# A hybrid decoder trunk on one core: the first mixer's chunk inverses over all four quadrants of TensorE, another order of scores, sums and weighing, and eight element-wise steps more on GpSimd

## What is computed

```python
def step(state, x):
    sa = jnp.einsum('bhij,bhj->bhi', state, a_t)
    state = state * w_t[:, :, None, :] + sa[..., None] * b_t[:, :, None, :] + v_t[..., None] * k_t[:, :, None, :]
    return state, jnp.einsum('bhij,bhj->bhi', state, r_t)
...
y = ((y - mean) * lax.rsqrt(var + RWKV_GN_EPS)).reshape(b_, s_, RWKV_WIDTH)
y = y * gn_w + gn_b
bonus = jnp.sum(r_h * k_h * r_k, -1, keepdims=True) * v_h
y = y.astype(cols.dtype) + bonus.reshape(b_, s_, RWKV_WIDTH)
return y * g
```

## Time and profile before

| | us |
|---|---|
| median of 3 runs | 1387.68 (1383.47 to 1388.83) |
| the profiled execution | 1384.46 |
| its span, first to last instruction | 1382.7 |

### The profile page before, as it was taken

The page is one execution under the profiler, slowest core; times in us unless marked ns, Lnnn a source line. Parts: engine busy times, 40 slices in busy tenths (PEclk is TensorE's granted clock), DMA queues, the critical chain, the costliest instruction groups (busy, mean ns, idle before and its releaser), DMA issues. The chain is left out here.

```text
span 1382.7 us, 20783 instructions
## 1 busy us (share of the span) xinstructions
PE 1252.7 (91%) x8752; PEld 701.5 (51%) x8752; DVE 408.8 (30%) x1019; ACT 269.8 (20%) x537; POOL 15.2 (1%) x18
## 2 busy tenths in 40 slices
PE   7999999899999888598899999998999998877986
PEld 4678874444444433243378888544444453333432
DVE  1158764511112111112135756224211211110211
ACT  2241440311110100010132566112111010000101
POOL 0000000000000000000000111000000000000000
PEclk9999999999999999889999999999999999997999
DMA  9620128999999999999964455958999999999996
GB/s 305 189 95 28 64 82 354 404 428 428 428 425 429 427 427 427 426 426 428 369 219 169 152 212 199 366 230 327 427 428 427 428 427 428 427 426 426 427 428 264
DMA packets 63482, 464.08 MB, mean 336 GB/s; under 512 B 8272, under 2 KB 13680, under 8 KB 34960
## 3 DMA queue, kind: packets, MB, share of 16 engines
q1 hardware_dynamic: 63376, 462.61, 81.8%
HBM read 461.51 MB, written 1.08 MB: 335 GB/s over the span
## 5 line engine op out<-in xcount | busy, mean ns | idle before, releaser
L1982 PE MATMUL bank<-raw,xg 128*32 128x512 f32 x1664 | 233.6, 654 | 46.9 <-DMA raw<-in_moe_w_up 41.1
L1892 DVE TENSOR_TENSOR aT<-bank,sg 128x128 f32<-128x128 f32 (+1 forms) x64 | 20.2, 316 | 553.9 <-ACT sg L1803 553.9
L1982 PEld LDWEIGHTS bank<-raw,xg 128*32 128x32 f32 x1664 | 57.9, 119 | 196.6 <-issue 122.0
L1919 PE MATMUL bank<-sel,ux 128*128 128x64 f32 (+1 forms) x896 | 117.7, 287 | 17.0 <-DVE sel L1825 16.1
L1919 PEld LDWEIGHTS bank<-sel,ux 128*128 128x128 f32 x896 | 110.9, 202 | 40.7 <-issue 21.6
L2029 PE MATMUL sums<-ys,selT 64*128 64x512 f32 x512 | 127.2, 615 | 3.3 <-DVE ys L1905 3.3
L1800 ACT COPY gus<-bank 128x512 f32<-128x512 f32 x64 | 37.5, 586 | 439.5 <-PE bank L1982 332.1
L2020 PE MATMUL bank<-raw,aT 128*32 128x512 f32 x832 | 100.0, 598 | 10.8 <-DVE aT L1892 10.8
L2029 PEld LDWEIGHTS sums<-ys,selT 64*128 64x128 f32 x512 | 44.1, 186 | 87.8 <-issue 80.9
L1963 PE MATMUL bank<-raw,xg 128*64 128x512 f32 x384 | 87.0, 594 | 0.0
L2623 PE MATMUL sums<-uT,wr 128*128 128x256 f32 x352 | 78.1, 380 | 0.0
(11 more groups left out here) (414 smaller groups left out, 1282.4 us busy)
## 6 DMA issues: line engine op xcount, KB each, us to landing
raw<-in_moe_w_gate SPq DMA_DIRECT2D x54, 2048.0 KB, 41.7
raw<-in_moe_w_up SPq DMA_DIRECT2D x54, 2048.0 KB, 46.1
raw<-in_moe_w_down SPq DMA_DIRECT2D x54, 2048.0 KB, 45.0
raw<-in_moe_w_gate SPq DMA_DIRECT2D x20, 1024.0 KB, 11.2
raw<-in_moe_w_up SPq DMA_DIRECT2D x20, 1024.0 KB, 12.7
raw<-in_moe_w_down SPq DMA_DIRECT2D x20, 1024.0 KB, 12.4
wr<-in_ssm_w_in SPq DMA_DIRECT2D x10, 2048.0 KB, 8.1
wr<-in_hyb_w_in SPq DMA_DIRECT2D x5, 2048.0 KB, 7.9
```

What stands on the lines that cost most here:

```text
L1892: V.tensor_tensor(out, bank[TURN_BANK][:, 0:8 * n].rearrange("p (j x) -> p j x", j=4)[:, :, n:2 * n], gated, ALU.mult).then_inc(S["act"], 1)
L1919: i = T.matmul(bank[SIDE_BANK][:, k * n:(k + 1) * n].rearrange("p (x s) -> p x s", x=2), ux[:, t, 4 * half + k, :], src[:, t, :, :], start ...
L1982: i = T.matmul(bank[GU_BANK][CAP_S * c:CAP_S * c + CAP_S, :], xg_f[:, x, 4 * half + k, :], raw[:, slot, k * FH:(k + 1) * FH], start=(half ...
```

## The change

1. `squares` takes both halves at once. For half t=1 tri and triT are kept with the partitions of the two chunks swapped (`crossed`), by a new multiplication "crossed" for triT and by products' output; so products and dT run over all four quadrants, and so do akv and wu. dTT stays with two. The first input of the second half, "at", is turned by eight 64-wide multiplications instead of four transposes.
2. gains of a chunk and queries of the next are given alternately.
3. In each round scores and products come before the turning and the attending; on VectorE the sums come before the weighing, and dT's sums before dTT's; on ScalarE products_read comes before weights_read.
4. The masks of rounds 1 to 4, three steps of pre and one of gate go to GpSimd; VectorE's last part and SyncE's next load wait for the last of them ("gain").

```diff
@@ VectorE, ahead of the rounds
-            did(V.tensor_tensor(triT, nrb[:, :, 0, :], rep(levT[:, 0], SL), ALU.mult))
+            go(V.tensor_tensor(triT[:, 0:HEADS, :], nrb[:, 0:HEADS, 0, :], rep(levT[:, 0], HEADS), ALU.mult))
+            dve.wait_ge(*at("crossed"))
+            for e in range(2):
+                go(V.tensor_tensor(triT[:, slot(1, e, 0):slot(1, e, 4), :],
+                                   bank_of("crossed", e)[:, 0:4 * CHK].rearrange("p (c s) -> p c s", s=CHK),
+                                   rep(levT[:, 0], 4), ALU.mult), "read", "crossed", e)
+            dve.wait_ge(dve_done, DV.n)
@@ VectorE, a round
-            masked(3)
-            dve.wait_ge(*got("par"))
-            go(V.tensor_tensor(pre, pre, rep(gn_b, HALVES), ALU.add))
             compressed_turned(1)
+            grown(3)
             weighted(4)
-            grown(3)
@@ GpSimd
+            def masked(l):
+
+                pool.wait_ge(*(at("prod", l - 1, 1) if l > 1 else at("lvl", 1)))
+                go(G.tensor_tensor(lv[:, (l + 1) % 2], nrb[:, :, 0, :], rep(levT[:, l + 1], SL), ALU.mult), "lvl", l + 1)
+
+            masked(1)
+            masked(2)
+            ...
+            go(G.tensor_tensor(pre, pre, gate[:, :, :], ALU.mult))
+            pool.wait_ge(pool_done, PO.n)
+            go(G.tensor_tensor(gate[:, :, :], gate[:, :, :], rep(gn_w, HALVES), ALU.mult), "gain")
@@ ScalarE, a round
+            products_read(4)
             attention_read(0)
             weights_read(4)
-            products_read(4)
@@ TensorE
-            def squares(b, g, left_, right_):
+            def squares(bs, left_, right_, source, to):
 
-                for s in range(HEADS):
+                for n in range(HEADS):
                     for q in range(2):
-                        i = T.matmul(b[at64(q), s * CHK:(s + 1) * CHK], left_[at64(q), HEADS * g + s, :],
-                                     right_[at64(q), HEADS * g + s, :], start=True, stop=True)
+                        for g in bs:
+                            i = T.matmul(bs[g][at64(to(g, q)), n * CHK:(n + 1) * CHK],
+                                         left_[at64(source(g, q)), HEADS * g + n, :],
+                                         right_[at64(source(g, q)), HEADS * g + n, :], start=True, stop=True)
                 return i
+
+            straight = lambda g, q: q
+            crossed = lambda g, q: q if g == 0 else 1 - q
 
             def products(l):
 
                 pe.wait_ge(*at("lvl", l))
                 if l == 1:
                     pe.wait_ge(*at("triT0"))
+                else:
+                    pe.wait_ge(*at("read", "dT", l - 1, 1))
+                bs = {g: take(pe, "prod", l, g, pool=right) for g in range(2)}
+                squares(bs, lv[:, l % 2], tri, straight, crossed).then_inc(pe_done, PE.one(("prod", l, 1)))
+
+            def grown(l):
+
+                pe.wait_ge(*at("read", "prod", l, 1))
+                if l > 1:
+                    pe.wait_ge(*at("read", "dTT", l - 1, 1))
+                if l < LAST:
+                    bs = {g: take(pe, "dT", l, g, pool=right) for g in range(2)}
+                    squares(bs, triT, prod, crossed, straight).then_inc(pe_done, PE.one(("dT", l, 1)))
                 for g in range(2):
+                    squares({g: take(pe, "dTT", l, g, pool=right)}, prod, triT, crossed, crossed).then_inc(
+                        pe_done, PE.one(("dTT", l, g)))
@@ TensorE, a round
-            weights_turned(4)
             scores(5)
             products(4)
+            attended(1)
+            weights_turned(4)
             grown(4)
@@ TensorE, behind the rounds
-            gains(0)
-            queries(1)
-            gains(1)
+            gains_queries(0)
             pe.wait_ge(*at("read", "wu", 1, 0))
             pe.wait_ge(*at("read", "wu", 1, 1))
-            gains(2)
-            queries(2)
-            queries(3)
+            gains_queries(1)
+            gains_queries(2)
             weights_turned(7)
```

More of the change, by code:

```diff
@@ L571, in _ @@
             sp.wait_ge(*at("attended", 3))
+            sp.wait_ge(*at("gain"))
             load_ahead(sp, 0, hyb_fed, hyb_attended)
@@ L791, in _ @@
                                        rep(pair, 4), ALU.mult), "read", "kar", t, e)
[L793 to L800 removed]
             def grown(l):
[L804 to L807 removed]
+                for name, dst in (("dT", tri), ("dTT", triT)):
+                    if name == "dT" and l == LAST:
+                        continue
+                    for g in range(2):
                         dve.wait_ge(*at(name, l, g))
@@ L1073, in _ @@
             exps(2)
+            products_read(2)
             weights_read(2)
-            products_read(2)
             exps(3)
@@ L1342, in _ @@
             against("bar", bh)
+            bs = [take(pe, "crossed", e, pool=right) for e in range(2)]
+            for c in range(4):
+                for e in range(2):
+                    for q in range(2):
+                        i = T.matmul(bs[e][at64(1 - q), c * CHK:(c + 1) * CHK],
+                                     bh[at64(e), c, chunk(1, q)], ar[at64(e), c, 0, chunk(1, q)], start=True, stop=True)
+            i.then_inc(pe_done, PE.one(("crossed",)))
             pe.wait_ge(*at("rk"))
@@ L1392, in _ @@
             grown(1)
+            scores(3)
+            products(2)
             attended(0)
             weights_turned(2)
-            scores(3)
-            products(2)
             compressed_out(0)
@@ L1436, in _, with gains_queries @@
             pe.wait_ge(*at("read", "at", 1))
-            for t in range(HALVES):
-                pe.wait_ge(*at("read", "dTT", LAST, t))
-                for e in range(2):
-                    b = take(pe, "wu", t, e, pool=right)
-                    for c in range(4):
-                        for q in range(2):
-                            i = T.matmul(b[at64(q), 2 * c * CHK:2 * (c + 1) * CHK], triT[at64(q), slot(t, e, c), :],
-                                         flat(xr_[at64(q), slot(t, e, c), :, :], "x", "s"), start=True, stop=True)
-                    i.then_inc(pe_done, PE.one(("wu", t, e)))
-            def gains(j):
+            pe.wait_ge(*at("read", "dTT", LAST, 1))
+            for e in range(2):
+                bs = [take(pe, "wu", t, e, pool=right) for t in range(HALVES)]
+                for c in range(4):
+                    for q in range(2):
+                        for t in range(HALVES):
+                            half = at64(crossed(t, q))
+                            i = T.matmul(bs[t][at64(q), 2 * c * CHK:2 * (c + 1) * CHK], triT[half, slot(t, e, c), :],
+                                         flat(xr_[half, slot(t, e, c), :, :], "x", "s"), start=True, stop=True)
+                i.then_inc(pe_done, PE.one(("wu", 1, e)))
+                new[("wu", 0, e)] = new[("wu", 1, e)]
+            def gains_queries(j):
                 t, q = j // 2, j % 2
-                b = take(pe, "g", j, pool=right)
+                t2, q2 = (j + 1) // 2, (j + 1) % 2
+                b, b2 = take(pe, "g", j, pool=right), take(pe, "qm", j + 1, pool=right)
                 for c in range(4):
```

117 lines of the change are left out of this document (53 added, 64 removed).

## The result

| | before | after |
|---|---|---|
| median | 1386.66 us (1383.47 to 1388.83, 4 runs) | 1375.51 us (1374.99 to 1377.71, 4 runs) |
| the profiled execution | 1384.46 us | 1377.71 us |
| its span | 1382.7 us | 1375.9 us |

The ratio is 0.9921, with a 95% interval from 0.9899 to 0.9943: faster by 0.8%. The forecast was 1381.3 us with a range from 1376 to 1388. The profiled execution took 1377.71 us where the sum gave 1378.1; the median lies 5.8 us under the forecast and 0.5 us under the range.

The account below looks back on a forecast made before the run. TensorE was taken to bound the rounds, VectorE close behind. Opening +2.2, rounds -9.2, end -0.95 and clock fall +1.6 sum to -6.35 us: 1378.1 for the profiled execution, 1381.3 for the median, range 1376 to 1388.

Parts of the forecast that it names:

- the rounds: First mixer's rounds: four-quadrant overlap and vanished waits, less two new waits, save 9.2 us.
- the akv wait: Round three: dTT wants akv's banks, which ScalarE empties only behind round four's exponentials, a new wait of 1.0 us.
- the new wait: Behind wu: TensorE waits about 2 us in front of the third gains-and-queries call.
- the adding: Opening: VectorE's adding of the identity, held by GpSimd's first mask, takes 2.7 us in place of 1.2.
- The opening, which gets longer: Up to the first scores: GpSimd's hold, crossed reads, turnings and clock add 2.2 us, bounds +0.5 and +3.5.
- The fall behind the new wait: After wu: TensorE's clock falls to half behind the wait before the third gains-and-queries call, costing 1.6 us.
- The base: Starting time: profiled execution 1384.46 us, the median of the runs 1387.68, 3.2 higher, added to the forecast.
- -0.95: End of the mixer: from wu's start to unit 7's turning takes 0.95 us less.
- rival 1: Opening and end: no fall of the clock and no holding, -8 to -10 us, 1378; chance 0.2.
- 2: Rounds: GpSimd also holds VectorE's PSUM-reading instructions, about 1 us per step reaches TensorE, +6, 1387.5 us; chance 0.15.
- 3: Rounds, wu and gains: four quadrants don't overlap because of a shared bank, +1, 1388.7 us; chance 0.07.
- 4: Rounds and opening: GpSimd's 128x1024 steps take longer, 5.5 us each, and delay the weighing, net +9, 1396.5 us; chance 0.08.

Follow-up runs that it names:

- e2: Changed kernel with the halves one after the other, only two quadrants alternating in products, dT, akv and wu: 1380.72 us, ratio 0.9962 to before.
- e6: Changed kernel with masks, bonus (pre) and gate steps back on VectorE: 1377.9 us, ratio 0.9945 to before.
- e3: Changed kernel with GpSimd's first mask waiting for VectorE's adding of the identity: 1375.53 us, ratio 0.993 to before.
- e9: Changed kernel with TensorE's opening waits filled by idle multiplications and GpSimd's first mask behind the identity's adding: 1375.64 us, ratio 0.9928 to before.
- e8: Changed kernel with idle multiplications in TensorE's two opening waits, first mask not moved: 1376.62 us, ratio 0.9939 to before.
- e13: Changed kernel again, no edit, a single profiled execution: 1375.04 us.
- e1: Changed kernel again, no edit, beside the kernel before: 1375.7 us, ratio 0.9935 to before.
- e7: Changed kernel with VectorE's weighing ahead of its sums again in all five rounds: 1379.29 us, ratio 0.9966 to before.
- e12: Changed kernel with e10's two orders, the first mask later, opening unfilled and a shorter filling at the end: 1370.38 us, ratio 0.9892 to before.
- e4: Changed kernel with two idle multiplications ahead of the third gains-and-queries call and two ahead of the last carried step: 1373.78 us, ratio 0.9922 to before.
- e10: Changed kernel with akv read ahead of unit 4's exponentials and unit 7's weights turned before the third gains-and-queries call: 1374.46 us, ratio 0.9916 to before.
- e14: Changed kernel again, no edit, a second single profiled execution: 1372.24 us.
- e5: Kernel before with two idle multiplications ahead of its last carried step: 1383.38 us, ratio 0.9988 to before.
- e11: Changed kernel with e9's filling and later mask, e10's two orders and the end filled: 1372.0 us, ratio 0.9903 to before.

## Why the prediction was right, and where it was wrong

**Right, with its numbers.** That TensorE sets the rounds and VectorE must get shorter with it: e2 and e6 show the two sides. Products 1.09 us forecast as 1.10, dT 0.98 as 1.10, a round of 7.14 us as 7.2, the akv wait 1.07 as 1.0, the turning's wait in round five 0.32 as 0.35 (and one more of 0.30 behind it, not walked), the new wait 1.98 as 2, unit 7's turning at 191.08 as 191.5, the adding 2.60 as 2.7, GpSimd's steps 2.36 us as 2.1 to 2.5. The Trainium skill's rule on banks and row tiles (TensorEngine Tiling (Array Packing), Gotcha 1: PSUM Pressure) would have kept products at 1.92 us; here two row halves wrote one bank, into different partitions, and the products took 1.09. Its rule on the lock (SBUF — State Buffer, Who interferes with whom) held on both sides: 2.60 us beside GpSimd and 1.23 without for two SBUF operands (e3).

**The opening, which gets longer: +2.2 us. Over-sized.** The four profiled executions of the changed kernel give +1.0, +0.75 and twice +0.05 (23.51, 23.23, 22.53, 22.53 against 22.48), 0.5 in the mean. I took GpSimd's hold (1.5) as lying on the path. It does not: TensorE has kar at half clock meanwhile, and e3 takes the hold away without winning anything; where the half clock is short, 0.4 us of it count (e9 against e8). The lower bound of +0.5 was the better value. TensorE's rows of kar (64x128) and of the first turning behind it (128x128) show what the sum left out, before, after and in e13, two rows each:

```profile
129.92 2.47 PE L1322 MATMUL sums<-front,qk 64*64 64x128 f32 x64
134.03 1.97 PE L1155 MATMUL sums<-cst,qk 128*128 128x128 f32 x8 [1.64 <-DVE wr L789]
132.03 3.69 PE L1339 MATMUL sums<-front,qk 64*64 64x128 f32 x64 [0.82 <-DVE kk L788]
135.66 1.97 PE L1172 MATMUL sums<-cst,qk 128*128 128x128 f32 x8
130.06 3.56 PE L1339 MATMUL sums<-front,qk 64*64 64x128 f32 x64 [0.82 <-DVE kk L788]
133.56 1.23 PE L1172 MATMUL sums<-cst,qk 128*128 128x128 f32 x8
```

With "crossed" ahead of it kar starts 2.1 us later behind the start of nn (15.59 and 15.60 against 13.46). Before, the turning waited 1.64 us for VectorE and came 4.11 us behind kar; now it comes 3.63 and 3.50 us behind it without a wait. From the turning to products of round one are 4.94 us before, 4.29 after and 3.43 in e13: with the delay of kar the length of the half clock decides between +1.0 and nothing. Of the eleven executions with the opening not filled six have the long one and 23.2 to 23.5 us (after, e1, e3, e6, e7, e12), five the short one and 22.5 (e2, e4, e10, e13, e14).

**The fall behind the new wait: +1.6 us. The size was right and the certainty wrong.** It is 1.4 to 1.7 us where it comes; it came in one of four profiled executions of the changed kernel (and in those of e3 and e6). It should have stood as a chance of one in four, 0.4 us; with e3, e6, e8 and e9, where the wait is also 1.98 us and nothing fills it, it came in three of eight. What decides whether it comes is not settled: the wait is 1.98 us in all four, with the same work ahead of it, and that it did not come with the wait filled (e4) is one execution. The old fall at the join, which I took for fixed, is missing in one of the four as well.

**The base: 1384.46 to 1387.68, "3.2 higher". Wrong.** I added the whole difference between the profiled execution and a median of three runs. Over 69 runs the median of before is 1385.49, 2.2 us lower.

These account for most of it: 2.2 of the base, 1.7 of the opening, 1.2 of the fall and 0.3 of the missing one at the join, together 5.4 us; the rounds, at 8.7 in place of 9.2, take 0.5 back, which leaves 4.9 of 5.8 us. The executions say the same in another way: mean length of the mixer 117.64 before and 108.26 after, -9.4 us, where my sum was -6.35; 1385.49 - 9.4 = 1376.1, and the 12 runs of the changed kernel have a median of 1375.34. The remaining 0.8 is within the scatter of what lies around the mixer (nn itself starts anywhere from 113.5 to 118.3 us, and the second expert layer's first piece takes from 3.5 to 6.3 us).

The first profiled execution of after happened to be the one with both falls and the long opening, which is why the sum fitted it to 0.4 us; that fit is luck. By its parts: opening +1.0 (forecast +2.2), rounds -8.7 (-9.2), end +0.5 (-0.95 and +1.6, so +0.65): -7.2 in the mixer (-6.35), two errors of different sign. The -0.95 itself is seen without the new fall: from the start of wu to unit 7's turning are 8.12 us in e1, e13 and e14, forecast as 8.25, where it was 9.19.

**The range.** Its low side, 1376, was set by rival 1 on the wrong base. Rival 1 (no fall, no holding in the opening) had 0.2. It describes what e13 and e14 show, in part by luck: no fall behind the new wait and no cost in the opening, though the holding was there (2.59 us for the adding in e13). e1 had no fall either, but +0.75 in the opening. On a base of 1385.5 it would have given 1376.

**The rest of the rivals.** 2 is out by 0.69 us a sum beside GpSimd, 3 by e2, 4 by GpSimd's 2.36 us a step: the three steps back to back never met a weighing that mattered.

## What to carry to other kernels

When work on a shared engine is made shorter, look at who is next: here the change has its full worth only with eight steps moved to an idle GpSimd (1.5 us, e6) and the sums put ahead of the weighing (3.3 us, e7). A forecast should subtract its difference from a base over many runs, and a clock that falls in some executions belongs in the chances and not in the sum; profiling the same kernel three or four times tells which events are fixed. An engine's hold or wait costs only what lies beyond the next slower one, so take it away in thought and ask who is late then.

## What was not expected of the hardware

- TensorE's granted clock fell in e8 with the engine busy by the profile in every window from 127 us on: it was at 1.00 at 128 to 129 us and at 0.50 from 130 on. Part of that busy time is instructions of two columns, so it does not say how much work was done. Filling the waits just ahead of it did not keep the clock up in three executions of three, while the four with the end filled (e4, e5, e11, e12) show no fall there; of the other fourteen, eleven have one at the join.
- The same program had no, one or two falls behind the rounds (106.84, 107.89 and 110.44 us for the same work), and two half-clock lengths in the opening, of about 4 and 6 to 7 us.
- GpSimd's steps of 128x1024 took 2.36 to 2.38 us, whether both inputs were full (pre times gate) or the second a row of 64 values repeated 16 times (the masks), but 1.90 where it was 16 values, each repeated 64 times in a row (the bonus); the one that met VectorE's instructions with two SBUF operands took 2.73.
- The first piece of the second expert layer took 3.50 us in one execution of the changed kernel and 6.34 in another, both behind a wait of 3.3 us, with a granted clock of 1.00 and 0.50: the whole 2.8 us by which the two executions differ.
